# A four-block sequence kernel: the state-space recurrence in steps of two, the last feed-forward by quarter products, the context read earlier

## The reference, cut to what matters

```python
# S5, for each of 64 groups with 64 complex states and 16 inputs
x[t] = A * x[t-1] + Bbar @ u[t]            # A = mag * exp(i*theta), diagonal
y[t] = Re(C @ x[t]) + d * u[t]
val, gate = split(gelu(y) @ w_glu + b_glu);  out = val * sigmoid(gate)
# modulation of the third and fourth block: 24 steps of 512 columns
mod = silu(c) @ ada_w[i] + ada_b[i]        # for the latent and the context vector
# attention's first step normalises x and the 256 context tokens
a = rms_norm(x) * (1 + scale) + shift
# a feed-forward, D 1024, F 2816
y = (silu(a @ w1) * (a @ w3)) @ w2
```

## Time and profile before

| | us |
|---|---|
| median of 3 executions (lowest, highest) | 2907.3 (2906.64, 2912.66) |
| the profiled execution, its time | 2906.8 |
| its span, first to last instruction | 2905.0 |
| TensorE busy | 2747.2 |
| VectorE busy | 774.5 |
| GpSimd busy | 638.2 |
| ScalarE busy | 393.9 |
| S5 recurrence | 601.7 to 754.5 |
| gate projection | 754.5 to 807.4 |
| experts | 850 to 1609.3 |
| ffn3 | 2668.8 to 2899.4 |

### The profile page before, as it was taken

The page is one execution under the profiler, slowest core; times in us unless marked ns, Lnnn a source line. Parts: engine busy times, 40 slices in busy tenths (PEclk is TensorE's granted clock), DMA queues, the critical chain, the costliest instruction groups (busy, mean ns, idle before and its releaser), DMA issues.

```text
span 2905.0 us, 50546 instructions
## 1 busy us (share of the span) xinstructions
PE 2747.2 (95%) x22403; PEld 1987.8 (68%) x22403; DVE 774.5 (27%) x1377; ACT 393.9 (14%) x775; POOL 638.2 (22%) x454
## 2 busy tenths in 40 slices
PE   7989999966889999999999799899999999999999
PEld 5846788822665565665555444558888878998888
...
GB/s 302 146 340 267 136 162 150 147 252 323 231 37 377 362 378 381 383 377 379 384 378 381 96 72 30 30 58 88 87 88 80 94 61 99 73 73 88 159 146 86
DMA packets 370053, 565.07 MB, mean 195 GB/s; under 512 B 48008, under 2 KB 203312, under 8 KB 369712
## 3 DMA queue, kind: packets, MB, share of 16 engines
...
HBM read 557.62 MB, written 1.05 MB: 192 GB/s over the span
## 4 chain that ended last, share of the span: by engine, by line
PE 55%; issue 34%; DVE 4%; DVEq 2%; DMA 2%; POOL 1%; POOLq 1%; ACT 1%; SPq 0%; ACTq 0%
PE psum L867 17%; PE psum L1597 9%; PE psum L977 5%; PE psum L1634 4%; PE psum L1676 3%; PE psum L1139 2%; PE psum L1696 2%; PE psum L1432 2%; DMA ring<-in_ada_w 2%; DVE xm L2604 1%; PE psum L1723 1%; PE psum L905 1%; POOLq L3192 1%; PE psum L1537 1%; DVEq L2588 1%
## 5 line engine op out<-in xcount | busy, mean ns | idle before, releaser
L1301 PE MATMUL psum<-ring,xe 128*32 128x256 f32 x8448 | 465.7, 380 | 0.0
L867 PE MATMUL psum<-act_in,ring 128*128 128x256 f32 x1920 | 423.5, 382 | 3.8 <-DVE act_in L2310 1.4
L867 PEld LDWEIGHTS psum<-act_in,ring 128*128 128x128 f32 x1920 | 368.2, 192 | 55.5 <-issue 4.3
L1301 PEld LDWEIGHTS psum<-ring,xe 128*32 128x32 f32 x8448 | 269.7, 110 | 182.6 <-issue 8.4
L1325 PE MATMUL psum<-ring,zs 128*32 128x256 f32 x4224 | 238.6, 381 | 5.4 <-ACT zs L2037 5.1
L3191 POOL TENSOR_TENSOR cq<-cq,nstat 128x512 f32<-128x512 f32 x3 | 3.7, 1268 | 937.3 <-DVE nstat L2807 937.3
L2731 DVE TENSOR_TENSOR zs<-zs,psum 128x128 f32<-128x128 f32 x132 | 37.7, 288 | 644.4 <-ACT zs L2033 644.4
L1325 PEld LDWEIGHTS psum<-ring,zs 128*32 128x32 f32 x4224 | 138.0, 110 | 97.3 <-issue 7.2
L3204 POOL TENSOR_TENSOR w_sums<-ring 128x512 f32<-128x512 f32 (+1 forms) x34 | 43.0, 1265 | 303.3 <-DVE ctxT L2858 132.8
L1432 PE MATMUL psum<-a,ring 128*128 128x512 f32 x224 | 98.3, 600 | 2.8 <-ACT a L2075 2.1
L2807 DVE RECIPROCAL nstat<-nstat 128x512 f32<-128x512 f32 x23 | 76.8, 3345 | 50.0 <-ACT nstat L1814 49.5
...
## 6 DMA issues: line engine op xcount, KB each, us to landing
...
```

Of the source, the lines that this page charges most:

```text
L867: last = pe.matmul(bank(j)[:, n * T:(n + 1) * T], tile[:, k * width + n * P:k * width + (n + 1) * P], src(k), start=start and k == 0, stop ...
L1301: last = pe.matmul(psum[32 * g:32 * g + 32, r, 0:2 * P].rearrange("p (u n) -> p u n", u=2), xe[:, 2 * i + k, at:at + 32], tile[:, k, :, g ...
```

## The change

**S5 in blocks of two steps.** The recurrence runs over the 128 odd steps with factor mag squared and twice the angle. Its input is B u at the odd step plus A B u at the even step before, so there is a second padded weight, `abpad`, made by GpSimd and turned on TensorE. Two pairs form a unit (16 units): VectorE's operations cover both pairs at 128 steps each, with four scans of 128. GpSimd turns forward with two products and then itself subtracts and adds the parts. Even outputs come from the state of the odd step before, through `caT` (C times A, six more GpSimd passes), and a direct term C B u through `direct`, made by 16 products in front of the first drive. There are three `zris` buffers.

**Six of the modulation steps** (18 to 23) move behind the recurrence, between the tiles of the gate projection, on SP and TensorE; the copies that need them move along. **The context** is loaded by SP right behind the last expert tile, into other memory, without `experts_done`; its squares and their sums come earlier. **ffn3** takes the seven-product form: x, hidden and each weight tile in quarters, 128 tokens a product, 34 tiles instead of 33, weight sums on GpSimd, joins on VectorE, the first product copied by ScalarE; the output is transposed in banks 4 to 7.

```diff
+GLU_ADA = {3: (18, 19), 4: (20,), 5: (21,), 6: (22, 23)}
...
+                def ada_c(s):
+
+                    l, at = divmod(s, ADA_BATCH["c"])
+                    for half in range(2):
+                        load_cols(ada_tile("c", s) + half, w["ada_w_2"][l], at * BANK, BANK, k0=4 * half, kc=4)
+
+                def glu(j):
+                    load_cols(glu_tile(j), w["s5_w_glu"][0], 256 * (j // 2) + D * (j % 2), 256)
+
+                for s in range(18):
+                    ada_c(s)
+                for j in range(3):
+                    glu(j)
+                for j, steps in GLU_ADA.items():
+                    for s in steps:
+                        ada_c(s)
+                    glu(j)
+                glu(7)
...
+                sp.dma_start(ctx_tok, w["ctx_2"][0].rearrange("(a p) d -> p a d", p=P)).then_inc(S("ctx_in"), 16)
 
             def stage_mla():
-                sp.wait_ge(S("experts_done"), 1)
-                sp.dma_start(ctx_tok, w["ctx_2"][0].rearrange("(a p) d -> p a d", p=P)).then_inc(S("ctx_in"), 16)
...
+                def drive(b):
+
+                    c, jobs = b // 2, unit_jobs(b)
+                    for j in jobs:
+                        wait_free(pe, j)
                     if b % 2 == 0:
                         pe.wait_ge(S("s5_u_ready"), c + 1)
                     for i in range(2):
-                        for p in (2 * b, 2 * b + 1):
-                            r, j = 32 * (p % 4), job_of["s_pair"] + p
-                            last = pe.matmul(bank(j)[:, i * T:(i + 1) * T], bT[r:r + 32, i, c], act_in[r:r + 32, c],
-                                             start=True, stop=True)
-                            if i:
-                                full(last, j)
+                        for e, held in enumerate((abT, bT)):
+                            for n in range(2):
+                                r = 32 * (2 * (b % 2) + n)
+                                last = pe.matmul(bank(jobs[n])[:, i * SB:(i + 1) * SB], held[r:r + 32, i, c],
+                                                 steps_of(act_in[r:r + 32, c])[:, e], start=e == 0, stop=e == 1,
+                                                 skip_group_check=True)
+                                if i and e:
+                                    full(last, jobs[n])
+
...
+                def direct_products():
+
+                    pe.wait_ge(S("cmT_ready"), 1)
+                    j = job_of["s_direct"]
+                    wait_free(pe, j)
+                    for b, dst in enumerate((bank(j), psum[:, NB + 1])):
+                        for c in range(4):
+                            for i in range(2):
+                                last = pe.matmul(dst[:, c * P:(c + 1) * P], bpad[:, i, 4 * b + c], cmT[:, i, 4 * b + c],
+                                                 start=i == 0, stop=i == 1)
+                        if b:
+                            last.then_inc(S("s5_y_full"), 1)
+                        else:
+                            full(last, j)
...
-                    if c >= 2:
-                        pe.wait_ge(S("s5_y_out"), c - 1)
-                    terms = ((cmT[:, 0], 0), (c_re_neg, 2), (cmT[:, 1], 1), (cmT[:, 1], 3))
-                    for n, (held, part) in enumerate(terms):
-                        for i in range(4):
-                            r = 32 * i
-                            last = pe.matmul(psum[r:r + 32, NB + c % 2, 0:T], held[:, c, r:r + 32], xparts[i][:, part],
-                                             start=n == 0, stop=n == 3)
+                        pe.wait_ge(S("cmT_ready"), 2)
+                    groups = [(32 * i, xparts[(2 * c + i // 2) % 4], i % 2) for i in range(4)]
+                    out = [psum[r:r + 32, NB + c % 2, 0:T] for r, _, _ in groups]
+                    for (r, _, _), y in zip(groups, out):
...
-                for c in range(DC):
-                    if c + 1 < DC:
-                        drive_two(2 * c + 2)
-                    ada_step("c", 3 * c + 2, 2)
-                    if c + 1 < DC:
-                        drive_two(2 * c + 3)
-                        ada_step("c", 3 * c + 3, 2)
...
+                ada_columns("c", 1, 2)
+                mm_pair(glu_tile(7), job_of["glu"] + 7, lambda k: gT[:, k])
                 layer_norm(2, lambda g: pe.wait_ge(S("ln_sum_ready"), 4 + g + 1))
 
             def stage_moe():
@@ -1420,7 +1537,14 @@
...
+                def context_sums():
+
+                    wait_free(pe, job_of["rms0"])
+                    pe.wait_ge(S("ctx_sq_ready"), 1)
+                    half_sums(job_of["rms0"], lambda c: rms_sq[:, c, T:T2], T, T2)
+                layer_norm(3, lambda g: pe.wait_ge(S("ln_sum_ready"), 8 + g + 1), between=context_sums)
...
+                def gate_up(n):
...
+                    quarter, sums, side = weight_quarters3(n), weight_sums3(n), gate_up_side3(n)
+                    operands = {1: (quarter[0, 0], lambda k: act_in[:, k, 0:P]),
+                                2: (quarter[0, 1], lambda k: act_in[:, 4 + k, 0:P]),
+                                6: (sums[1], lambda k: x_sums3[:, 1, k]),
+                                5: (sums[0], lambda k: x_sums3[:, 0, k]),
+                                7: (sums[2], lambda k: act_in[:, k, P:T]),
+                                3: (sums[3], lambda k: act_in[:, 4 + k, P:T]),
...
+                        if n == 0 and m in (6, 7, 4):
+                            pe.wait_ge(S("x_sums_ready"), 8 + {6: 2, 7: 3, 4: 4}[m])
+                        for k in range(4):
+                            if n == 0 and m in (1, 2):
+                                pe.wait_ge(S("a2_lat_ready"), 24 + (0 if m == 1 else 4) + k + 1)
+                            last = pe.matmul(small_bank(side, m), held[:, k], moving(k), start=k == 0, stop=k == 3)
+                            if m == 1 and k == 0:
+                                last.then_inc(tile_begun, 1)
+                        if m == 6:
...
+                            act.wait_ge(S("down_out"), 4 + q + 1)
+                        act.wait_ge(S("down_full"), 16 + 4 * half + 2 * q + 1)
+                        act.activation(first_prod3[:, q], small_bank(down_side3(half, q), 1), ACT.Copy).then_inc(S("first_out"), 1)
...
+                def unit(b):
+
+                    jobs = unit_jobs(b)
+                    dve.drain()
+                    for j in jobs:
+                        wait_full(dve, j)
+                    at = jobs[0] % NB
+                    v = psum[:, at:at + 2, 0:T].rearrange("p n (k t) -> p k n t", k=2)
+                    zri = zris[b % 3]
+                    z, zt = of_pairs(zri), of_pairs(ztmp)
+                    sin = turn(1, b)
+                    if b < 2:
+                        dve.wait_ge(S("x_kept"), 2 * b + 2)
+                    elif b > 2:
+                        dve.wait_ge(S("s5_x_ready"), b - 2)
+                    dve.tensor_tensor(zt[:, 0], v[:, 1], sin[:, 0], ALU.mult)
+                    dve.scalar_tensor_tensor(zt[:, 1], v[:, 0], -1.0, sin[:, 0], ALU.mult, ALU.mult)
+                    out_of(dve.tensor_tensor(z, v, turn(0, b), ALU.mult), jobs[0])
+                    out_of(dve.drain(), jobs[1])
                     dve.tensor_tensor(zri, zri, ztmp, ALU.add)
                     dve.drain()
-                    mag_t = sv[:, 3, bass.ds(p, 1)].broadcast_to([P, SL])
-                    for k in range(2):
-                        last = dve.tensor_tensor_scan(zri[:, k], mag_t, zri[:, k], 0.0, ALU.mult, ALU.add)
+                    for n in range(2):
+                        mag_t = sv[:, 3, 2 * b + n:2 * b + n + 1].broadcast_to([P, SB])
+                        for k in range(2):
+                            last = dve.tensor_tensor_scan(z[:, k, n], mag_t, z[:, k, n], 0.0, ALU.mult, ALU.add)
                     last.then_inc(S("s5_z_ready"), 1)
...
+                def y_out(c):
+
+                    dve.wait_ge(S("s5_y_full"), c + 2)
+                    dve.scalar_tensor_tensor(gT[:, c].rearrange("p (t e) -> p t e", e=2),
+                                             act_in[:, c].rearrange("p (t e) -> p t e", e=2), col("s5_d", c),
+                                             psum[:, NB + c % 2, 0:T].rearrange("p (e t) -> p t e", e=2), ALU.mult, ALU.add
...
-                        dve.wait_ge(S("ffn3_sum"), c // 2 + 1)
-                    dve.scalar_tensor_tensor(xT[:, c], psum[:, NB + c // 2, (c % 2) * T:(c % 2 + 1) * T],
-                                             mod[:, 3, 40 + c, 0:1], xT[:, c], ALU.mult, ALU.add).then_inc(S("x_final"), 1)
+                x11, x12, x21, x22 = act_in[:, 0:4, 0:P], act_in[:, 0:4, P:T], act_in[:, 4:8, 0:P], act_in[:, 4:8, P:T]
+                dve.drain()
+                dve.tensor_tensor(x_sums3[:, 0], x12, x11, ALU.subtract).then_inc(S("x_sums_ready"), 1)
+                dve.drain()
+                dve.tensor_tensor(x_sums3[:, 1], x22, x_sums3[:, 0], ALU.subtract).then_inc(S("x_sums_ready"), 1)
```

(71 more changed lines are left out.)

431 lines of the change are left out of this document (289 added, 142 removed).

## The result

The changed kernel takes 2862.9 us (median of four runs, 2855.3 to 2864.9) against 2909.4 before (2906.6 to 2912.7): 0.9835 of it, 95% interval 0.9813 to 0.9857. The prediction was 2851, in the range 2830 to 2875. The profiled execution took 2863.0, its span 2861.2, which is 43.8 less than the span before where 55.9 were forecast.

A forecast was written before the change was run, and what follows sets the result against it. TensorE was taken to bound most of the kernel (95% busy), GpSimd and VectorE taking turns the state-space stage. Terms -52.1 + 3.5 + 0.7 + 15.5 - 8 - 15.5 = -55.9 gave 2851 us, range 2830 to 2875.

The forecast's parts named there:

- Rival A: Recurrence: nothing interleaves, GpSimd's four operations, then VectorE's whole unit, 7.7 us a unit; +24, total 2875; chance 0.13.
- rival B: Recurrence: turns cheaper than thought and the queue leads at 5.5 us a unit; total 2840; chance 0.10.
- the unit: Recurrence: two pairs at 128 steps take 6.2 us, 6.1 of turns plus 0.1 of hand-over.
- 2 x 1.27 + 2 x 0.725 = 3.99: Recurrence: GpSimd's time per unit in us, two 512 products and two new 256 sums.
- the gate projection: Stage behind the recurrence: moved modulation steps, column products and tile waits, less a shorter read-out, +15.5; with the exit's +0.7, +16.2.
- The steps (11.2) and columns: Gate projection: six modulation steps moved into TensorE's full stretch cost 11.2 us, their column products 1.1.
- rival E: Recurrence: its gain is handed back because weights can't come sooner; at most +9.5, total 2861; chance 0.05.
- lie in ffn0 under TensorE's full stretch: ffn0: VectorE's extra parameter steps and GpSimd's second pad cost nothing; only the transposes add, +1.75.
- rival C: ffn3: GpSimd's weight sums lead at 6.7 us a tile; +15, total 2866; chance 0.12.
- D: ffn3: each 128-column product costs its two weight loads in full, 0.384 us; +148, total 2999; chance 0.02.
- the tail: End of ffn3, behind the last product: five joins and two updates for both q instead of one pair of updates, +2.1.
- the entry: Before the recurrence: direct products and GpSimd passes meeting VectorE; +1.75 here, +3.5 together with ffn0's transposes.

The follow-up runs named there:

- its own experiment: The changed kernel with the context loaded after the experts and its square sums in the common ones, as before: 2871.1 us, ratio 0.9861.

## Why the prediction came out as it did

**Right in the mechanism.** The bound of the recurrence was read correctly: GpSimd and VectorE take turns, PSUM readers do not take part, TensorE and the queue lie under it. Rival A (7.7 a unit) is excluded by the measured 5.43. The experiment with half the loads excludes that the queue leads, so rival B is right in its first half (the turns are cheaper) and wrong in its second.

**Mis-sized: the unit, 6.2 for 5.43.** The step that failed is "2 x 1.27 + 2 x 0.725 = 3.99", together with taking what takes turns as the sum of whole instruction lengths. The scans were right (1.41 for 1.37). The sums cost 0.84 instead of 1.45, the addition 0.54 instead of 0.69. My reading, which no run tests by itself, is that the part of a short instruction's recorded length in which it does not hold the shared resource lies beside the other engine's instruction. The Trainium skill, "SBUF — State Buffer", section "Who interferes with whom", says that a VectorE instruction with two SBUF inputs contends with a GpSimd instruction that reads SBUF, and that the one that comes second blocks until the first is done. Which instructions collide agrees with this trace. Full blocking by whole lengths would give 2.54 + 0.69 + 1.45 + 1.37 = 6.05, and 5.43 was measured. 15 x 0.77 is 11.6, and the recurrence gained 11.4 over the forecast.

**Mis-sized the other way: the gate projection, +16.2 for +27.6.** The steps (11.2) and columns were right. Three things failed. First, I asked whether the queue leads a unit (5.5 against 6.2) and, finding that it does not, took it as harmless; at 5.43 a unit it was full (361 GB/s from 630 to 680, 386 from 680 to 700), so the last modulation tiles came late, SP could ask for the first glu tile only at 693.0, and it landed at 705.78. So the seven eighths of its products that need no late chunk, which before ran from 744.1 to 752.0 beside the recurrence, stand behind it: 6.3. Second, the waits are 1.58 + 1.36 + 1.95 + 1.50 = 6.39 instead of 4.3. Third, the clock behind two of these waits, 2.6 + 1.7, which I had priced at nothing. 12.1 + 6.3 + 6.4 + 4.3 - 1.1 for the read-out = 28.0, for 27.6 measured. This is rival E's mechanism (the gain is handed back because the weights come no sooner), and it took just what the cheaper turns gave. I had bounded it by +9.5, from a sum over tiles that left out the slots of the ring. They count: after its request at 702.78 SP gets only three more out until 730.07, from 714 to 730 the queue moves 86 GB/s, and two tiles begun instead of three gave 3.9 back. With half the modulation's loads the projection takes 69.4, next to the 69.1 that the forecast gives (52.9 + 16.2). So the sum for the two stages came out right because the queue took back what the cheaper turns gave, which I had not foreseen; that this sum holds is luck on my side.

**Wrong: ffn0, +1.75 for +9.3.** The step is the sentence that the extra parameter steps on VectorE "lie in ffn0 under TensorE's full stretch". They do, but VectorE works in order, and behind them stands the product of halves for which TensorE waits. In the trace of before, the end of that chain, the product of halves behind it and TensorE's next down projection already stood with no slack between them:

```profile
420.36 0.46 DVE L2528 TENSOR_TENSOR sv<-sv 128x32 f32<-128x32 f32 x2
421.31 0.69 DVE L2332 TENSOR_TENSOR zs<-zs,psum 128x512 f32<-128x512 f32 x1 [0.49 <-issue]
...
422.26 7.07 PE L977 MATMUL psum<-zs,ring 128*128 128x256 f32 x32
```

Twelve steps longer, the chain stops TensorE, and the clock falls behind the pause. From ScalarE's first operation on log_dt to TensorE's down projection 10.3 us pass before the change (411.94 to 422.26), and 13.7 in each of the ten profiles that have the longer chain in this place. So the chain is worth 3.4 us of pause. The rest depends on when log_dt lands, which was between 411.0 and 418.0: the pause was 1.9 where ScalarE could begin 11.8 us ahead of TensorE, and 5.95 where it began 7.8 ahead. ffn0 took 249.5 to 255.1 in these ten. With the chain two steps later it took 246.1 to 247.8, in three profiles. To price an addition to an in-order engine at nothing, one must read the slack of the instruction behind it, not only how busy the other engine is.

**ffn3: -15.0 for -17.6 in the stretch.** The product count and 0.2235 a product were right: a tile takes 6.25 in steady state, and no weight sum is waited for there, so rival C and D fall. The short tile 27 costs the next one 1.57 where 1.5 was forecast. What was missed is the clock at the start:

```profile
2644.17 3.75 PE L1946 MATMUL psum<-x_sums,w_sums 128*128 128x128 f32 x16 [0.85 <-DVE x_sums L3317]
2647.71 3.01 PE L1946 MATMUL psum<-act_in,w_sums 128*128 128x128 f32 x16
...
2653.24 1.95 PE L1946 MATMUL psum<-x_sums,w_sums 128*128 128x128 f32 x16
```

16 records take 3.75 and 3.01 here, 1.95 from then on. The granted clock is 0.50, the lower of TensorE's two levels, up to 2644, and 0.61 in the mean from there to 2651.5; tile 0 waits for VectorE's sums in this stretch (0.85 in the first line). These two groups cost 2.9 us more than at full clock, on top of the 4.4 that were forecast, and tile 0 lost 7.2 in all. No run separates the gaps in tile 0 from the pauses just before ffn3 as the cause of that clock. GpSimd did stretch when it met VectorE, as the earlier trace rows had it (1.73 instead of 1.31), and still had 0.34 to 0.86 to spare in the tiles up to 2671:

```profile
2658.01 1.30 POOL L3589 TENSOR_TENSOR w_sums<-ring 128x512 f32<-128x512 f32 x1 [0.86 <-PE psum L1946]
2659.28 1.73 POOL L3590 TENSOR_TENSOR w_sums<-ring 128x512 f32<-128x512 f32 x1
```

**The rest.** The early context (-7.6 in the profiles, 8.2 by its own experiment, -8 forecast), the tail (+2.0 for +2.1) and the entry (+2.1 for +1.75, one meeting of VectorE with GpSimd's pass, in which two operations that take 0.73 together elsewhere took 2.80) were right. The first, sixth and eighth stage of the table moved by +1.9, -2.5 and +1.9 although no work of theirs was changed. The first one lay between 339.0 and 343.6 over all profiles; why these three moved stays open. The total was right within its range because two errors of 11 us cancel; what is left is mainly ffn0.
